# Layer 1's first four query chunks moved to the end of layer 0's FFN, with the adaLN units behind them

## What is computed

```python
x = _layer_norm(ALPHA * x + ml[5] * _swiglu(...), ln_g[l, 1], ln_b[l, 1])      # end of layer 0
...
h_lat = _modulate(x, ml[0], ml[1])                                            # layer 1
qk, v, og, g = jnp.split(h @ w_in, [o1, o2, o3], axis=-1)
qk = jax.nn.silu(_centred_conv(qk, conv_w, conv_b))
q, k = jnp.split(qk, 2, axis=-1)
```

## Time and profile before

| | us |
|---|---|
| median of 3 runs | 1898.49 |
| lowest, highest | 1891.13, 1899.65 |
| profiled execution, its own time | 1890.27 |
| its span on the core | 1888.5 |
| PE busy in the span | 1773.1 (94%) |
| DVE, ACT, POOL busy | 687.6, 611.1, 715.9 |
| share of the last-ending chain on PE | 82% |
| mean granted TensorE clock | 0.972 |

### The profile page before, as it was taken

How to read it: one execution, slowest core, us unless ns; L and a number is a source line. 1 busy time by engine, 2 the same in 40 slices (tenths; PEclk the granted TensorE clock), 3 DMA queues, 4 the chain that set the end, 5 groups by cost and what they waited for, 6 DMA issues and landing times.

```text
span 1888.5 us, 24473 instructions
## 1 busy us (share of the span) xinstructions
PE 1773.1 (94%) x9848; PEld 1427.0 (76%) x9848; DVE 687.6 (36%) x1187; ACT 611.1 (32%) x869; POOL 715.9 (38%) x378
## 2 busy tenths in 40 slices
PE   4999999899899999999999996999976999999998
PEld 2788767455487888888888883887765888888886
DVE  2134345666557611110111126470178661111114
ACT  0531322555434422121211225342333453122124
POOL 0442200166445533323332243243334754445435
PEclk9999999999899999999999997999988999999999
DMA  8411232355312222212211126221200323333222
GB/s 297 122 45 56 67 123 90 100 168 179 112 48 65 67 65 69 64 48 67 76 58 55 45 67 208 56 67 56 79 1 23 95 79 95 111 89 104 86 83 73
DMA packets 212010, 163.36 MB, mean 86 GB/s; under 512 B 17742, under 2 KB 191022, under 8 KB 211926
## 3 DMA queue, kind: packets, MB, share of 16 engines
q1 hardware_dynamic: 209344, 157.77, 27.9%
q10 hardware_dynamic: 2582, 4.42, 0.6%
HBM read 160.08 MB, written 2.10 MB: 86 GB/s over the span
## 4 chain that ended last, share of the span: by engine, by line
PE 82%; DVE 10%; ACT 3%; issue 2%; DMA 1%; POOL 1%; ACTq 0%; POOLq 0%; DVEq 0%
PE ps L700 59%; PE ps L688 3%; PE ps L690 3%; PE ps L689 3%; PE ps L862 2%; PE ps L889 2%; PE ps L914 1%; PE ps L800 1%; PE ps L899 1%; PE ps L816 1%; DMA ring<-in_mod_w 1%; DVE xT L2013 1%; PE ps L652 1%; DVE xT L2003 1%; PE ps L642 1%
## 5 line engine op out<-in xcount | busy, mean ns | idle before, releaser
L2387 POOL TENSOR_TENSOR wsplit<-ring,wsplit 128x1024 fp32r<-128x1024 f32 (+1 forms) x136 | 326.0, 2411 | 523.5 <-ACT wsplit L1471 523.2
L700 PE MATMUL ps<-hhi,wsplit 128*128 128x512 f32 (+1 forms) x1920 | 475.4, 355 | 6.4 <-DVE hu L2052 6.4
L700 PEld LDWEIGHTS ps<-hhi,wsplit 128*128 128x128 f32 x1920 | 317.7, 189 | 58.6 <-DVE hu L2052 6.9
L700 PE MATMUL ps<-hlo,wsplit 128*128 128x512 f32 x960 | 289.1, 355 | 0.0
L700 PE MATMUL ps<-uhi,wsplit 128*128 128x512 f32 x1008 | 250.6, 353 | 0.0
L2129 DVE TENSOR_TENSOR hu<-sg,ps 128x768 f32<-128x768 f32 (+1 forms) x40 | 32.9, 821 | 440.6 <-ACT sg L1540 440.6
L1471 ACT ACTIVATE wsplit<-ring 128x1024 fp32r<-128x1024 f32 (+1 forms) x136 | 135.2, 1024 | 173.5 <-PE ps L700 173.5
L700 PEld LDWEIGHTS ps<-uhi,wsplit 128*128 128x128 f32 x1008 | 165.8, 188 | 26.8
L700 PEld LDWEIGHTS ps<-hlo,wsplit 128*128 128x128 f32 x960 | 159.0, 189 | 25.9
L1976 DVE SCALAR_TENSOR_TENSOR xT<-ps,modc,xT 128x512 f32<-128x512 f32 x96 | 60.6, 659 | 273.2 <-PE ps L700 251.7
L700 PE MATMUL ps<-ulo,wsplit 128*128 128x512 f32 x504 | 151.0, 353 | 0.0
(11 more groups left out here) (369 smaller groups left out, 2705.5 us busy)
## 6 DMA issues: line engine op xcount, KB each, us to landing
ring<-in_mod_w SPq DMA_DIRECT2D x96, 512.0 KB, 4.9
ring<-in_ffn_w_in SPq DMA_DIRECT2D x88, 512.0 KB, 3.8
ring<-in_ffn_w_out SPq DMA_DIRECT2D x32, 512.0 KB, 4.1
ring<-in_m_w_in SPq DMA_DIRECT2D x24, 512.0 KB, 3.8
ring<-in_ab_w_in SPq DMA_DIRECT2D x21, 512.0 KB, 3.9
ring<-in_ffn_w_out SPq DMA_DIRECT2D x16, 384.0 KB, 3.4
ring<-in_ab_w_out SPq DMA_DIRECT2D x8, 512.0 KB, 4.8
ring<-in_m_w_out SPq DMA_DIRECT2D x8, 512.0 KB, 3.9
```

Source lines behind the costliest of these rows:

```text
L700: mm = pe.matmul(dst[:, a:b], w, h[:, a:b], start=st, stop=sp_)
L2387: pool.tensor_tensor(w_part(s, 1)[:, 0:width], ring[:, (NB[f"ffn{l}"] + s) % RING, 0:width], w_part(s, 0)[:, 0:width].bitcast(F32), ALU.su ...
```

## The change

Units 0 to 3 of the projection enter the ring directly behind the FFN's last unit, as four more FFN units (`N_FX`), split by `ffn_split` and `ffn_low` into `wsplit`. f0 and f1 (`N_Q`) become late products from the residual: ACT makes `zqhi` and DVE `zqlo` behind each residual update, PE multiplies (L1091), and DVE evaluates them later in `late_query`, into `cacc`, from where ACT's `conv_in` adds the shift. ACT still splits two units behind the seventh and the eighth chunk of `next_input`, now units 4 and 5. f2 and f3 run chunk by chunk on `hlo1`, with one adaLN unit between chunks; the gate product stands alone behind them and behind both `late_query`, because f1 is in `PS[3]`. Of the 16 adaLN units, three go to a buffer of their own (`mod_pre`) during the FFN, and 13 stand in the ring between unit 3 and unit 4 of the projection. The sums of the norm stand behind f0. The bank of each chunk is given by `q_bank`.

The diff, cut to its core:

```diff
+    QW = LAT + 2
+    zqhi, zqlo, mod_pre = under(("zqhi", [P, KD, QW], F32R), ("zqlo", [P, KD, QW], F32R), ("mod_pre", [P, 3, UNIT], F32))
...
+    N_FX, N_Q, MOD_PRE = 4, 2, 3
     STAGES = (("mod00", KD), ("mod01", KD), ("in0", N_IN0), ("mod03", KD), ("mod04", KD), ("mod02", KD), ("mod10", KD),
-              ("mod11", KD), ("mod05", KD), ("mod14", KD), ("mod15", KD), ("out0", N_OUT), ("ffn0", N_FFN), ("mod12", KD), ("mod13", KD), ("in1", N_IN1),
+              ("mod11", KD), ("mod05", KD), ("mod14", KD), ("mod15", KD), ("out0", N_OUT), ("ffn0", N_FFN + N_FX), ("mod12", KD - MOD_PRE), ("mod13", KD), ("in1", N_IN1 - N_FX),
...
+    def q_bank(f):
+
+        return PS[(2, 3, 0, 1, 2, 0, 1, 2)[f]]
+
+    def q_made(f):
+
+        return FT[0] + N_FFN + f + 1 + TILE_CREDIT
...
-        mod_units(1, 2)
+        sp.wait_ge(ffn_tile, FT[0] + N_FFN - KD + TILE_CREDIT)
+        for k in range(MOD_PRE):
+            sp.dma_start(mod_pre[:, k, :], mod_w[1, k * P:(k + 1) * P, 2 * D:3 * D]).then_inc(mod_pre_in, 16)
+        w_in = m_w_in[0].rearrange("(k p) n -> p k n", p=P)
+        for i in range(N_FX):
+            n = NB["ffn0"] + N_FFN + i
+            slot_free(n)
+            unit(n, view(n % RING, KD), w_in[:, :, i * P:(i + 1) * P])
+        mod_units(1, 2, MOD_PRE)
...
+        pe.wait_ge(zq_cols, 1)
         pe.wait_ge(z_ev, ZB[1] - 1)
-        mod_rows_stacked(1, 2, half(4), 0, 3)
-        ln_sums(1)
-        mod_rows_stacked(1, 2, half(4), 3, KD)
-        mod_rows_stacked(1, 3, half(5))
-
+        for f in range(N_Q):
+            pe.wait_ge(lo_made, FB[0] + N_FFN + f + 1)
+            if f == 1:
+                pe.wait_ge(z_ev, ZB[1])
+            for k in range(KD):
+                if f == 0:
+                    pe.wait_ge(zq_lo, k + 1)
+                for w, z, st, sp_ in ((0, zqhi, k == 0, False), (0, zqlo, False, False), (1, zqhi, False, k == KD - 1)):
+                    for a, b, at in LATE_MM[1]:
+                        mm = pe.matmul(q_bank(f)[:, at:at + b - a], w_part(f, w)[:, k * P:(k + 1) * P], z[:, k, a:b], start=st, stop=sp_)
+            mm.then_inc(ffn_tile, 1)
+            if f == 0:
+                ln_sums(1)
+
+
+        rows2, rows3 = PS[0][:, T:], PS[1][:, T:]
+        pe.wait_ge(ln_mean, 2)
+        pe.wait_ge(ln_var, 2)
+        pe.wait_ge(mod_pre_in, 16 * MOD_PRE)
+        for k in range(MOD_PRE):
+            for b in range(4):
+                pe.matmul(rows2[32 * b:32 * b + 2, :], s_kv[:, k, :], mod_pre[:, k, 256 * b:256 * (b + 1)], start=(k == 0), stop=False)
+        mod_rows_stacked(1, 2, rows2, MOD_PRE, KD - 1)
 
         def m_chunk(f, k):
-            w_hi, w_lo = (w[:, f % 2, k * P:(k + 1) * P] for w in (whi1, wlo1))
-            return project(PS[f % 3], w_hi, w_lo, hT1[:, k, :], hlo1[:, k, :], k == 0, k == KD - 1,
+            w_hi, w_lo = (w_part(f, a)[:, k * P:(k + 1) * P] if f < N_FX else (whi1, wlo1)[a][:, f % 2, k * P:(k + 1) * P] for a in range(2))
+            return project(q_bank(f), w_hi, w_lo, hT1[:, k, :], hlo1[:, k, :], k == 0, k == KD - 1,
                            ALL_SEGS if f >= 4 else ALL_SEGS[:1])
 
-        pe.wait_ge(ln_rstd, 2)
-        pe.wait_ge(z_ev, ZB[1])
-        for k in range(KD + 2 * LAG):
+        rest = [(1, 2, rows2, KD - 1)] + [(1, 3, rows3, k) for k in range(KD)]
+        for k in range(KD + LAG):
             if k < KD:
                 pe.wait_ge(input_lo, 2 * KD + k + 1)
-            for f, kf in ((0, k), (1, k - LAG)):
+            for f, kf in ((2, k), (3, k - LAG)):
                 if 0 <= kf < KD:
                     if kf == 0:
-                        split_unit("in1", f)
+                        pe.wait_ge(lo_made, FB[0] + N_FFN + f + 1)
                     mm = m_chunk(f, kf)
                     if kf == KD - 1:
-                        mm.then_inc(unit_done, 1)
-            kf = k - 2 * LAG
-            if 0 <= kf < KD:
-                if kf == 0:
-                    pe.wait_ge(gate_lo, 1)
-                mm = project(PS[3], wg[:, 0, kf, :], wg[:, 1, kf, :], hT1[:, kf, :], hlo1[:, kf, :], kf == 0, kf == KD - 1, ALL_SEGS)
-                if kf == KD - 1:
-                    mm.then_inc(gate_mm, 1)
-        mod_columns(1, 2, half(4))
-        for f in range(2, 8):
-            if f == 2:
+                        mm.then_inc(ffn_tile, 1)
+            if k < len(rest):
+                l, g, rows, n = rest[k]
+                mod_rows_stacked(l, g, rows, n, n + 1)
+        pe.wait_ge(gate_lo, 1)
+        pe.wait_ge(late_q, 2)
+        for k in range(KD):
+            mm = project(PS[3], wg[:, 0, k, :], wg[:, 1, k, :], hT1[:, k, :], hlo1[:, k, :], k == 0, k == KD - 1, ALL_SEGS)
+        mm.then_inc(gate_mm, 1)
+        mod_columns(1, 2, rows2)
+        for f in range(4, 8):
+            if f == 5:
+                mod_columns(1, 3, rows3)
                 pe.wait_ge(mod_ev, MOD_AT[1, 2])
-            if f == 5:
+            if f == 6:
                 pe.wait_ge(mod_ev, MOD_AT[1, 3])
-            if f >= 3:
+            if f >= 5:
                 pe.wait_ge(f_ev, f - 2)
-            if f == 3:
-                mod_columns(1, 3, half(5))
             split_unit("in1", f)
             for k in range(KD):
                 mm = m_chunk(f, k)
             mm.then_inc(unit_done, 1)
         in1_parts = ((whi1, wlo1), hT1, hlo1)
-        token_major("in1", 8, [(t, t) for t in (4, 5, 0, 1, 2, 3)], *in1_parts, lambda b: pe.wait_ge(f_ev, (7, 8, 6)[b // 2]))
+        token_major("in1", 8, [(t, t) for t in range(TT)], *in1_parts, lambda b: pe.wait_ge(f_ev, (6, 7, 8)[b // 2]))
         pe.wait_ge(gate_ev, 4)
         pe.wait_ge(rows_ok, 1)
         for d in range(2):
...
-            if i >= 2:
+            if i >= (N_FX + 2 if stage == "in1" else 2):
...
+                if i == 2 and k == 0:
+                    act.wait_ge(ffn_tile, q_made(N_Q - 1))
...
+                    if third == 2 and l == 0:
+                        if m == 0:
+                            act.wait_ge(gains_ok, 2)
+                        act.activation(zqhi[:, m, 0:LAT], xT[:, m, 0:LAT], ACT.Copy, scale=gain[:, 1, 0, m, 0:1]).then_inc(zq_hi, 1)
+                        if m == KD - 1:
+                            split_static(N_FFN + 2, UNIT)
...
-        from_norm(1, hT1, hlo1_raw, lambda i: split_high("in1", i, whi1))
+        from_norm(1, hT1, hlo1_raw, lambda i: split_high("in1", i + N_FX, whi1))
...
         def conv_in(f):
-            if f >= 2:
+            if f >= 4:
                 split_high("in1", f + 2, whi1)
-            act.wait_ge(unit_done, UB["in1"] + f + 1)
-            if f < 2:
+            if f < N_Q:
                 act.wait_ge(pad_ok, 4)
+                act.wait_ge(late_q, f + 1)
+                act.activation(cpad[:, f, 1:1 + LAT], cacc[:, f, 0:LAT], ACT.Identity, bias=qc[:, f, 1:2]).then_inc(f_ev, 1)
+                return
+            if f < N_FX:
+                act.wait_ge(ffn_tile, q_made(f))
             else:
-                act.wait_ge(conv_done, f - 1)
-            ins = act.activation(cpad[:, f % 2, 1:1 + LAT], PS[f % 3][:, 0:LAT], ACT.Copy)
+                act.wait_ge(unit_done, UB["in1"] + f + 1)
+            act.wait_ge(conv_done, f - 1)
+            ins = act.activation(cpad[:, f % 2, 1:1 + LAT], q_bank(f)[:, 0:LAT], ACT.Copy)
             if f >= 4:
-                ins = act.activation(cpad[:, f % 2, LAT + 3:T + 3], PS[f % 3][:, LAT:T], ACT.Copy)
+                ins = act.activation(cpad[:, f % 2, LAT + 3:T + 3], q_bank(f)[:, LAT:T], ACT.Copy)
...
-        conv_in(0)
-        split_high("in1", 3, whi1)
+        for f in range(N_Q):
+            conv_in(f)
+        act.wait_ge(gate_mm, 1)
+        for g, dst in enumerate((li, gt, li, gt)):
+            act.activation(dst[0:H_M, g // 2, :], PS[3][32 * g:32 * g + H_M, 0:T], ACT.Identity,
+                           bias=gb[32 * g:32 * g + H_M, :]).then_inc(gate_ev, 1)
...
-        for f in range(1, 8):
+        for f in range(2, 8):
             conv_in(f)
-            if f >= 2:
-                conv_out(f - 2)
+            conv_out(f - 2)
...
+        def zq_low(m):
+            dve.wait_ge(zq_hi, m + 1)
+            dve.scalar_tensor_tensor(zqlo[:, m, 0:LAT], xT[:, m, 0:LAT], gain[:, 1, 0, m, 0:1], zqhi[:, m, 0:LAT].bitcast(F32),
+                                     ALU.mult, ALU.subtract).then_inc(zq_lo, 1)
+
+        def zq_columns():
+            g_, b_ = gain[:, 1, 0, :, 0], gain[:, 1, 1, :, 0]
+            step(dve.tensor_scalar(zqhi[:, :, LAT], g_, -1.0, None, ALU.mult))
+            step(dve.tensor_copy(zqhi[:, :, LAT + 1], b_))
+            dve.scalar_tensor_tensor(zqlo[:, :, LAT], g_, -1.0, zqhi[:, :, LAT].bitcast(F32), ALU.mult, ALU.subtract)
+            dve.tensor_tensor(zqlo[:, :, LAT + 1], b_, zqhi[:, :, LAT + 1].bitcast(F32), ALU.subtract).then_inc(zq_cols, 1)
+
+        def late_query(f):
+
+            dve.wait_ge(ffn_tile, q_made(N_FX - 1))
+            step(dve.tensor_copy(qc[:, f, :], q_bank(f)[:, LATE_COL[1]:LATE_COL[1] + 2]))
```

(22 more changed lines are left out.)

56 lines of the change are left out of this document (28 added, 28 removed).

## The result

The changed kernel took 1899.62 us (median of 20 runs, 1891.62 to 1907.94), the kernel before, run beside it, 1893.70 (20 runs, 1882.70 to 1899.65). The ratio is **1.0043**, 95% interval 1.0026 to 1.0060: some 8 us (5 to 11) slower; the two medians themselves differ by 5.9. A second series gave 1.0043 again (1.0022 to 1.0065). The forecast, 1899.0 in the range 1887.5 to 1906.5 and within 0.5%, holds by its number, and that is partly luck: the forecast stood on 1898.5 for the kernel before, the median of three runs, and over twenty runs that kernel is at 1893.7. The difference foretold was +0.5 us and is +8.1 by the ratio.

The account below looks back on a forecast made before the run. PE, busy 94%, bounds the kernel: +3.3 us (norm), +6.1 (ring) and the rest to the gates, 10.1 in all; -13.4 for two fewer chunks; +4.3 for DVE; about +0.5 on 1898.5, so 1899, range 1887.5 to 1906.5.

Parts of the forecast that it names:

- The norm: Layer seam: the sums end at 1154.6 instead of 1151.35 behind late product f0, making the norm 3.3 us later.
- the idle time ahead of the loop: Before the chunk loop: PE idle 3.3 us, as the first remainder is ready at 1167.1 instead of 1163.76.
- the low clock behind it: Start of the chunk loop: the low clock counted on for the first two passes after PE's idle time.
- ACT's wait at unit 4: Between ACT's seventh and eighth chunk: the split waits for a transfer landing at 1182.8; ACT idle 5 to 7 us.
- the wait for DVE's convolutions: Inside the first token-major unit: PE waits 4.3 us for conv_in(7), from 1247.5.
- The ring: Chunk loop: pass of 1.9 us, transfer issued at 1179, landing 3.8 us later; 6 us of the last remainder's delay.
- the slow case: Slow-ring rival: landing takes up to 7.9 us, deciding from 4.5 us on; 6 us slower, 1904.5; chance 0.17.
- PE's tail behind the last remainder: End of the chunk loop: 3.7 us of work at full clock, half of 5 us lost; f3 ends at 1193.1.
- The late evaluation: Between f3 and the gates: both late_query take 5 us, between 3.5 clean and 6.8 with both multiplies blocked.
- The unit behind PE's wait: First token-major unit: 5.6 us left after PE's wait, ending at 1257.4 by one count, 1254.9 by another.
- the ring holds ACT longer: Rival at unit 4's split: eighth chunk 4.1 us later, gates end at 1214.8, 6 us slower, 1904.5; chance 0.17.
- Hidden work: FFN's updates: the zqhi and zqlo cuts hide under 6.2 us products; uncovered, each step would cost 0.75 or so.

Follow-up runs that it names:

- c2: c1 with the norm's sums on PE moved into the first late product, ahead of its seventh chunk; ratio to the kernel before 0.9924, second series 0.9927.
- e1: c2 with tiles 4 and 5 in the gates' PSUM bank, plus POOL centring ahead of its low part of the fourth query chunk's weights; ratio 0.9935.
- a1: Changed kernel with ACT's high parts of ring units 4 and 5 moved behind the gate weights' copies; ratio to the kernel before 0.9992.
- a4: Changed kernel with all thirteen adaLN ring units read by PE ahead of the chunk loop, none between passes; ratio to the kernel before 1.0000.
- a2: Changed kernel with POOL waiting for both late evaluations before its low parts of units 4 and 5; ratio to the kernel before 1.0009.
- c1: a3 with the late evaluation cut in two, only the multiply by lnr waiting for f3, and gates waiting for chunk 1's alone; ratio 0.9937.
- a3: Changed kernel with the edits of a1 and a2 together; ratio to the kernel before 0.9994.

## Why the prediction was right, and where it was not

On one scale, in us behind the FFN's last product; what was foretold is the prediction's clock less 1145.7. The step's own error is what it adds to the error of the steps ahead of it.

| step | foretold | measured | the step's own error |
|---|---|---|---|
| second sum ends | 8.9 | 8.5 | -0.4 |
| first remainder ready | 21.4 | 21.8 | +0.8 |
| unit 4's transfer issued | 33.3 | 34.9 | +1.2 |
| landed | 37.1 | 39.5 | +0.8 |
| last remainder ready | 41.2 | 43.6 | 0.0 |
| f3 ends | 47.4 | 50.8 | +1.0 |
| gates start | 52.4 | 57.8 | +2.0 |
| gates end | 63.2 | 68.9 | +0.3 |
| `conv_in(7)` out, PE goes on | 106.1 | 110.6 | -1.2 |
| first unit ends | 111.7 | 117.9 | +1.7 |

**The steps in their order were right.** The norm 2.9 us later by its sums, the idle time ahead of the loop (4.5 instead of 3.3), the low clock behind it, ACT's wait at unit 4 with chunk, gate weights and PE queued behind, the long late evaluation, 36.1 us (35.8) from the gates to the token-major units, and the wait for DVE's convolutions inside the first of them. Each is in the rows above.

**Five sizes were too small.** (1) The norm, 0.8: in the kernel before the first remainder was ready 12.4 us behind the second sum, now 13.3. DVE's first operation on the sums starts 0.37 us behind them (0.04 before), and the next takes longer, before and after:

```profile
1152.38 1.08 DVE L2000 TENSOR_SCALAR lnbuf<-lnbuf 128x768 f32<-128x768 f32 x1
```

```profile
1157.66 1.63 DVE L2057 TENSOR_SCALAR lnbuf<-lnbuf 128x768 f32<-128x768 f32 x1
```

It starts 0.6 us behind the first of POOL's centrings (before: 1.2) and in both kernels ends 2.3 us behind that start, as if it waited for the centring. POOL comes to it right behind its two new low parts. The three centrings on DVE take as long as before (4.34, 4.30); in c2 and e1 they are what is stretched. (2) The ring, 1.2 and 0.8: a pass takes 2.12 us and not 1.9, the pace of ACT, which delivers a chunk in 2.08, so over six passes the transfer is issued 1.3 us later. Here I misread my own rows: I had ACT's 2.09 from the earlier trace rows and set the pass against DVE's 1.74. And the transfer took 4.65 us to land (issued at 1182.67, split at 1187.32), where I took the median of 3.8. The prediction had the slow case decide from 4.5. (3) PE's tail behind the last remainder, 1.0: the clock stayed low for most of it (a mean of 0.56 from 1186.9 to 1198.6). (4) The late evaluation, 2.0: at 6.95 us it is the upper bound of 6.8, with both multiplies blocked, where I took 5. POOL and DVE are released by the same product of f3, so the block is no matter of chance: from f3's end to the gates it is 6.9 to 7.0 us in all four profiles with this order (the changed kernel's two, a1, a4). a2 shows it, and 3.68 without it, against the 3.5 of the lower bound. (5) The unit behind PE's wait, 1.7: 7.4 instead of 5.6, at a clock lowered once more.

With 0.3 at the gates they sum to 7.8; less 0.4 and the 1.2 by which the convolutions' chain is shorter than I had it, 6.2: the unit ends at 117.9 instead of 111.7. The line of the kernel before is at 110.9, so +7.0 instead of the +0.5 to +1. The rival "the ring holds ACT longer" had the gates' end at 69.1 (68.9) and the unit's end at 116.3 to 117.3 (117.9); it had a chance of 0.17.

**What failed was the choice between the bounds**, beside the pass that was misread. For the landing and the late evaluation the rows gave both ends; I took the median and the middle. But these ends were not independent draws. The slower loop made the transfer late, the late transfer made the idle time long, and behind the idle time the clock was low; and the release shared by POOL and DVE blocked each time. In this chain the costs went to their upper ends together.

**The absolute time** came out within 0.7 us by luck, from two errors that cancel: the median of before is 4.8 us lower over twenty runs than over three, and the medians lie 5.9 us apart instead of 0.5.

**The range** held the time; the claim "within 0.5%" holds by the median ratio, 0.43%, and with nothing to spare: the interval goes up to 0.60%.

**Hidden work.** The cuts for `zqhi` and `zqlo` cost nothing, as said: in the FFN's last third the updates stand 6.24 us apart with them, at the pace of 579 (DVE's updates in e1 begin at 1133.40 and 1139.64).

## What to carry to other kernels

A split, copy or cast that needs a transfer does not belong between two steps of a chain on an in-order engine, however little it costs itself: put it behind the chain's last step, and only the transfer's own reader waits (8.8 us here, by moving two splits). When a wait of the matmul engine is cut, look at the clock behind it: 2.8 us of idle time taken away gave 5.0. And when a sum is made of bounded unknowns that stand in one chain, ask which of them go up together before taking the middle of each. The pace of a loop is that of the slowest engine in it (ACT's 2.08 us a chunk here), whatever the others could do.

## What the runs showed that I had not expected

- The pace of steady matmuls has two values at the same granted clock of 1.00: 579 or 568 records in 100 us, 6.24 or 6.36 us for the same product of the FFN, in runs of the same chip and of nearly the same code. The 35 runs of the kernel before beside a1 to a4 fall into two bunches, 16 at 1882 to 1889 us and 19 at 1892 to 1901. These may be the two paces, which put the FFN's end some 10 us apart, but only profiled runs show a pace, and the FFN's start moves too, by up to 7.5 us from profile to profile; so it is not shown.
- The same wait of 2.2 us within the first token-major unit had a low clock behind it in both profiles of the changed kernel, in a1 to a4 and in one profile of c2 (the unit ends 7.3 to 7.4 us behind it), and none in c1 and the other profile of c2 (5.8 to 5.9). The 3.68 us ahead of the gates of a2 and a3 had one, the 0.88 of c1 to e1 none in six profiles.
- POOL's low part itself takes 2.40 us at f3's end, where DVE's multiply is the one that waits. The low part of a query unit, of the same shape, takes 5.17 for two in c2 and 3.12 for one in e1, where it follows POOL's centrings while DVE centres: there POOL seems to wait too.
